# Six ring slots instead of eight, and one weight chunk of the gating unit kept for both token blocks

## The chip, the cores and the metric

One core of one Trainium2 chip runs the kernel. The time is the device time of one execution in microseconds. Before: 1674.19 us, the median of three runs (1673.43 to 1676.97).

## The reference

A decoder trunk of two layers on 256 tokens of width 1024, all in float32. Layer 0 mixes tokens by stick-breaking attention and gated linear attention, layer 1 by a gated unit; behind each stands a retrieval of single-neuron experts (PEER). Cut to what the change touches:

```python
def layer_c(h, w_in, v_norm, w_spatial, b_spatial, w_out):
    z = gelu(h @ w_in)                      # w_in: 1024 x 4096
    u, v = split(z, 2)
    v = rmsnorm(v, v_norm)                  # in chunks of 128 tokens, 8 groups
    mixed = einsum('gts,bnsgc->bntgc', causal(w_spatial), v) + b_spatial
    return (u * mixed) @ w_out

def peer(h, w_q, subkeys, u_tab, v_tab):
    ...                                     # 8 heads x top 16 = 128 experts per token: idx, gate
    act = gelu(einsum('td,tkd->tk', x, u_tab[idx]))
    return einsum('tk,tkd->td', gate * act, v_tab[idx])
```

Every token needs 128 rows of `u_tab` and 128 rows of `v_tab`, which the kernel keeps side by side as one row of 2048 floats.

## The kernel before

The 256 tokens are two blocks of 128, one token to a partition. The work stands in a list of stages, `PLAN` (line 191), which each engine walks in the same order and of which it takes its own part; semaphores join them.

**The gather loop.** A PEER of one block is 128 steps, four such loops in a row: layer 0 block 0, layer 0 block 1, layer 1 block 0, layer 1 block 1, in all 512 steps. In a step GpSimd issues an indirect DMA (line 543) that gathers one expert's row for each of the 128 tokens into a slot of `ring`, 128 x 2048 floats. VectorE multiplies the first half with `h` and sums (line 1043), ScalarE makes the gelu, scales it by the gate and writes a diagonal matrix (lines 718, 719, 721), and TensorE multiplies that with the second half of the slot into the accumulators `acc` (line 1363), which frees the slot (`rows_used`). The ring has `SLOTS` = 8 slots, and `dots`, `gelus` and `diag` have as many. GpSimd waits before step t until step t - 8 is used:

```python
if t >= SLOTS:
    pool.wait_ge(rows_used, t - SLOTS + 1)
```

**What runs between the steps.** `gather_with` (line 95) sets other stages behind given steps: behind the steps of layer 0 block 0 the query products of both blocks (`parts_of_layer0`), behind those of layer 0 block 1 the whole layer 1 trunk of block 0 (`trunk_for(0)`), behind those of layer 1 block 0 the trunk of block 1 and further query products (`trunk_for(1)`, `parts_for(0)`). TensorE does all this in its one queue with the gather's matmuls.

**The weights.** All weights come in chunks of 1024 x 512 floats, 128 x 4096 on the chip, into a double buffer `weights`, issued by SyncE (`load_chunk`, line 420): chunk n waits until chunk n - 2 has been used. The input weights of the gating unit are 8 chunks, `c_w_in[0]` to `c_w_in[7]`. A block uses them in the order 4, 5, 6, 7, 0, 1, 2, 3 (`ZPROJ` and `ZMORE` in `trunk_for`, TensorE's helper `tall`, line 1144), so each is loaded twice, once for each block: 16 loads. One chunk, the first of the query weights, lies in `z` instead (`first_chunk`), without the double buffer.

**The ring before the loops.** While layer 0 mixes, the ring's 8 x 2048 floats per partition hold its intermediate tiles (`slots(k)`, k = 0 to 15 in halves of a slot); the halves 12 to 15 hold `v_g`, `gg`, `og` and `scT`.

Of the kernel before, what the change touches and what calls it, by code (L numbers as in the profile page):

```python
# [19 lines left out]
NEG = -1.0e30  # L20
LOWEST = -3.0e38

SLOTS = 8
STEPS = NE
PARTS = 4
PHEADS = PH // PARTS
# [53 lines left out]
def chunks_of(kind, args):  # L80

    if kind == "QPROD":
        layer, b, m, heads = args
        return int(layer == 1 or (b == 0 and not first_chunk_holds(layer, m)))
    return {"PROJQK": 2, "PROJV": 1, "MIX0": 5, "ZPROJ": 1, "MIXO": 2}.get(kind, 0)


ALL = tuple(range(PHEADS))
# [30 lines left out]
def projected(at, layer, b, m, gap=2):  # L119

    q = (layer, b, m, ALL)
    done = at + gap * (TILES - 1) + 1
    return ([(at, ("QPROD", *q))] + [(at + gap * i, ("QMORE", *q, i)) for i in range(1, TILES)]
            + [(done, ("QTAKE", *q)), (done + 1, ("QDOT", *q)), (done + 3, ("DTAKE", *q))])
# [51 lines left out]

def parts_of_layer0():

    return (projected(0, 0, 0, 1) + projected(10, 0, 1, 1, 4) + ranked(11, 0, 0, 2, 2) + projected(16, 0, 0, 2)
            + ranked(23, 0, 0, 3, 2) + projected(26, 0, 1, 2, 4) + projected(33, 0, 0, 3) + ranked(36, 0, 0, 4, 2)  # L180
            + projected(46, 0, 1, 3, 4) + ranked(48, 0, 0, 5, 2) + projected(62, 0, 1, 0, 4) + ranked(60, 0, 0, 6, 2)
            + ranked(72, 0, 0, 7, 2) + ranked(84, 0, 1, 0, 2) + ranked(96, 0, 1, 1, 2) + ranked(108, 0, 1, 2, 2)
            + ranked(120, 0, 1, 3))
# [60 lines left out]
def trunk(nc, x_in, cols, gains, ab_w_in, ab_w_rank, ab_w_alpha2, ab_w_out, c_w_in, c_v_norm, c_spatial, c_w_out,  # L244
# [6 lines left out]
    with ctx:  # L251
# [9 lines left out]
        hT = sb("hT", [P, KT, T])  # L261
        mixT = sb("mixT", [P, KT, T])
        weights = sb("weights", [P, 2, KT, CH])
        ring = sb("ring", [P, SLOTS, 2 * D])
        z = sb("z", [P, 2 * SGW])
        scores = sb("scores", [P, 2 * PH * NK])
        scores1 = sb("scores1", [P, 2 * PH * NK])
# [36 lines left out]
        def slots(k, n=1):  # L304
            return ring[:, :, :].rearrange("p a b -> p (a b)")[:, k * D:(k + n) * D]

        first_chunk = z[:, :].rearrange("p (k n) -> p k n", n=CH)

        suffix = slots(9)[:, 768:768 + 2 * P].rearrange("p (a b) -> p a b", a=2)
# [28 lines left out]
        chunk_in = [sem(f"chunk_in{k}") for k in range(2)]  # L338
        half_used = sem("half_used")
        first_chunk_in = sem("first_chunk_in")  # L340
        out_full = sem("out_full")
        x_in_sem = [sem(f"x_in{b}") for b in range(NBLK)]
        consts_in = sem("consts_in")
# [67 lines left out]
        @block.sync  # L411
        def _(sp):
            norms = 0
            norms_with = {}
            chunk_free = []

            def filled(n):
                return full[n % WB], n // WB + 1

            def load_chunk(n, src, used):  # L420
                if n >= 2:
                    sp.wait_ge(*chunk_free[n - 2])
                sp.dma_start(weights[:, n % 2, :, :], src).then_inc(chunk_in[n % 2], 16)
                chunk_free.append(used)

            halves_used = 0
            for kind, args, at in walk():
                bank, chunk = at.bank, at.chunk
                if kind == "COLS":
                    sp.dma_start(consts[:, :], cols).then_inc(cols_in, 16)  # L430
                elif kind == "NORM":
                    name = args[0]
                    if name in GAIN_SLOT and name not in norms_with:
                        if name == "final":
                            sp.wait_ge(h_ready, norms_with["ffn0"])
                        src = gains[("ffn0", "ffn1", "final").index(name)]
                        slot = GAIN_SLOT[name][0]
                        sp.dma_start(gain[:, slot, :], src.partition_broadcast(P)).then_inc(gain_in[slot], 16)
                    norms += len(args[1])
                    norms_with[name] = norms  # L440
                elif kind == "PROJQK":
                    for j in range(2):
                        load_chunk(chunk + j, ab_w_in[j], filled(bank + 2 * j + 1))
                    sp.dma_start(w_rank[:, :, :], ab_w_rank).then_inc(consts_in, 16)
                elif kind == "PROJV":
                    load_chunk(chunk, ab_w_in[2], filled(bank + 1))
                elif kind == "MIX0":
                    for j, (part, last) in enumerate(((3, B_GK), (5, B_GG1), (4, B_GV1))):
                        load_chunk(chunk + j, ab_w_in[part], filled(bank + last))
                    for n in range(2):  # L450

                        load_chunk(chunk + 3 + n, ab_w_out[n], (out_full, 3 + n))
                elif kind == "GLAREAD":
                    sp.wait_ge(*filled(bank + 1))
                    sp.dma_start(first_chunk, peer_w_q[0, 0]).then_inc(first_chunk_in, 16)
                elif kind == "SPATIAL":
                    sp.dma_start(spatialT[:, :, :], c_spatial).then_inc(spatial_in, 16)
                elif kind == "QKEYS":
                    if args[0]:
                        sp.wait_ge(*filled(BANKS["QDOT", 0, 1, 0, ALL]))  # L460
                    sp.dma_start(keysT[:, :, :], peer_keys[args[0]]).then_inc(keys_in, 16)
                elif kind == "QPROD" and not first_chunk_holds(args[0], args[2]):
                    layer, b, m, heads = args
                    if layer == 1:
                        load_chunk(chunk, peer_w_q[layer, m], filled(bank))
                    elif b == 0:
                        load_chunk(chunk, peer_w_q[layer, m], filled(BANKS["QPROD", layer, 1, m, heads]))
                elif (kind, *args) == ("VNORM", 0):
                    sp.dma_start(v_norm[:, :], c_v_norm.partition_broadcast(P)).then_inc(v_norm_in, 16)
                elif kind == "ZPROJ":  # L470
                    load_chunk(chunk, c_w_in[args[1]], filled(bank))
                elif kind == "MIXO":
                    halves_used += 1
                    for kh in range(2):
                        load_chunk(chunk + kh, c_w_out[kh, args[1]],
                                   filled(bank) if kh else (half_used, halves_used))
                elif kind == "FINISH":
                    for n in range(2):
                        sp.wait_ge(h_ready, norms + n + 1)
                        sp.dma_start(out[0, (NBLK - 1) * P:, n * CH:(n + 1) * CH], h[:, NBLK - 1, n * CH:(n + 1) * CH])\  # L480
                            .then_inc(stored, 16)
                elif kind == "STORE":
                    sp.wait_ge(h_ready, norms)
                    sp.dma_start(out[0, args[0] * P:(args[0] + 1) * P, :], h[:, args[0], :]).then_inc(stored, 16)
            sp.wait_ge(stored, 16 * (NBLK + 1))

        @block.gpsimd
        def _(pool):
# [32 lines left out]
            for kind, args, at in walk():  # L521
# [14 lines left out]
                elif kind == "GATHER":  # L536
                    layer, b, i0, i1 = args
                    for step in range(i0, i1):
                        t = first_step(layer, b) + step
                        pool.wait_ge(experts_ready, 1 + IDS_ORDER[layer, b, step // TOPK])  # L540
                        if t >= SLOTS:
                            pool.wait_ge(rows_used, t - SLOTS + 1)
                        pool.indirect_dma_start(  # L543
                            ring[:, step % SLOTS, :], None, uv_rows,
                            bass.IndirectOffsetOnAxis(ap=experts[:, b, step:step + 1], axis=0))\
                            .then_inc(row_in[step % SLOTS], 16)

        @block.scalar
        def _(act):
# [108 lines left out]
            for kind, args, at in walk():  # L658
# [54 lines left out]
                elif kind == "GATHER":  # L713
                    layer, b, i0, i1 = args
                    for step in range(i0, i1):
                        k = step % SLOTS
                        act.wait_ge(dots_done, first_step(layer, b) + step + 1)
                        link(nc.scalar.activation(gelus[:, k:k + 1], dots[:, k:k + 1], ACT.Gelu))  # L718
                        link(nc.scalar.activation(gelus[:, k:k + 1], gelus[:, k:k + 1], ACT.Copy,  # L719
# [35 lines left out]
        def _(dve):  # L755
# [216 lines left out]
            for kind, args, at in walk():  # L972
# [64 lines left out]
                elif kind == "GATHER":  # L1037
                    layer, b, i0, i1 = args
                    for step in range(i0, i1):
                        k = step % SLOTS  # L1040
                        t = first_step(layer, b) + step
                        dve.wait_ge(row_in[k], 16 * (t // SLOTS + 1))
                        nc.vector.tensor_tensor_reduce(  # L1043
# [58 lines left out]
        def _(pe):  # L1102
# [40 lines left out]

            def tall(n, chunk, src, b, q=0, pieces=1):

                wt = await_chunk(pe, chunk)
                w = work[n % WB] if q else claim_bank(pe, n)
                for k in range(q * KT // pieces, (q + 1) * KT // pieces):
                    last = nc.tensor.matmul(w[:, :], src[:, k, b * P:(b + 1) * P], wt[:, k, :],  # L1149
# [150 lines left out]
            for kind, args, at in walk():  # L1300
# [56 lines left out]
                elif kind == "GATHER":  # L1357
                    layer, b, i0, i1 = args
                    for step in range(i0, i1):
                        pe.wait_ge(diag_ready, first_step(layer, b) + step + 1)  # L1360
                        k = step % SLOTS
                        for n in range(2):
                            last = nc.tensor.matmul(acc[2 * b + n][:, :], diag[:, k, :],  # L1363
                                                    ring[:, k, D + n * CH:D + (n + 1) * CH],
                                                    start=False, stop=True, skip_group_check=True)
                        last.then_inc(rows_used, 1)
                elif kind == "ZPROJ":
                    tall(bank, chunk, hT, args[0], 0, Z_PIECES)
                elif kind == "ZMORE":
                    tall(bank, chunk, hT, args[0], args[2], Z_PIECES)  # L1370
                elif kind == "MIXG":
                    b, k = args
                    pe.wait_ge(spatial_masked, 1)
# [57 lines left out]
```

## Time and profile before

| | before |
|---|---|
| median of 3 runs | 1674.19 us |
| the profiled execution's own time | 1672.77 us |
| span of its trace | 1671.0 us |
| TensorE matmul busy | 1440.7 us, 86% |
| VectorE busy | 983.1 us, 59% |
| ScalarE busy | 681.5 us, 41% |
| GpSimd busy | 658.7 us, 39% |
| moved by DMA | 637.54 MB, mean 382 GB/s |
| granted TensorE clock, mean | 0.969 of full speed |

The span runs from the first to the last instruction of the program; the profiled execution's time lies 1.8 us above it. A busy share is an average over stages with different limits. The share of the DMA engines is a mean over the core's 16 engines.

### The profile page before, as it was taken

How to read it: one execution, taken by the hardware profiler on the slowest of the kernel's cores; microseconds unless marked ns; L12 is line 12 of the kernel's file. 1: busy time of each engine (PE TensorE's matmuls, PEld its weight loads, DVE VectorE, ACT ScalarE, POOL GpSimd, SP SyncE). 2: the span in 40 equal slices, each digit the busy share in tenths (PEclk: the TensorE clock that was granted, in tenths of full speed). 3: DMA queues.
4: the chain of work that ended last, by engine and by line, in shares of the span. 5: the costliest groups of instructions: out<-in, count | busy, mean ns of one | idle time of the engine just before them, and what ended most of it. 6: DMA issues, size and time to landing. Idle time of an engine off the chain costs nothing.

```text
span 1671.0 us, 14524 instructions
## 1 busy us (share of the span) xinstructions
PE 1440.7 (86%) x4326; PEld 705.8 (42%) x4326; DVE 983.1 (59%) x2484; ACT 681.5 (41%) x1854; POOL 658.7 (39%) x537
## 2 busy tenths in 40 slices
PE   6999799998777988998888897989888897897786
PEld 5665466653222333443334444444334343342222
DVE  1132666776778755643446755664554785777654
ACT  1672334453345534333334433533334452544433
POOL 1000244464464433344244342424333553445673
PEclk9999799999899999999999999999999998999999
DMA  5323799999999999999999999999999999999996
GB/s 205 112 101 113 294 369 421 412 422 423 421 422 421 423 421 423 420 423 423 421 421 422 391 422 421 398 401 394 422 422 422 421 420 424 421 421 421 421 421 263
DMA packets 82190, 637.54 MB, mean 382 GB/s; under 512 B 9264, under 2 KB 9408, under 8 KB 10560
## 3 DMA queue, kind: packets, MB, share of 16 engines
q0 software_dynamic: 73728, 536.90, 77.8%
q1 hardware_dynamic: 8064, 98.65, 14.3%
q10 hardware_dynamic: 320, 1.07, 0.2%
q8 instruction: 34, 0.56, 0.1%
q14 instruction: 44, 0.36, 0.1%
HBM read 635.53 MB, written 1.05 MB: 381 GB/s over the span
## 4 chain that ended last, share of the span: by engine, by line
PE 41%; DMA 38%; DVE 8%; ACT 5%; issue 5%; POOL 4%; DVEq 0%; POOLq 0%; ACTq 0%
DMA ring<-in_peer_uv,experts 35%; PE acc L1363 22%; PE work L1149 7%; PE work L1164 6%; DVE ring L1043 4%; POOL ring L543 4%; PE work L1139 2%; PE acc L1328 1%; DMA weights<-in_c_w_in 1%; ACT diag L721 1%; ACT gelus L719 1%; DMA weights<-in_peer_w_q 1%; PE work L1347 1%; DMA x<-in_x 1%; ACT gelus L718 1%
## 5 line engine op out<-in xcount | busy, mean ns | idle before, releaser
L1363 PE MATMUL acc<-ring,diag 128*128 128x512 f32 x2048 | 983.2, 616 | 181.1 <-ACT diag L721 179.6
L543 POOL DMA_INDIRECT ring<-in_peer_uv,experts x512 | 648.8, 1267 | 872.7 <-PE acc L1363 721.7
L1043 DVE CUSTOM_DVE_ANT_0 ring<-ring,h 128x1024 f32<-128x1024 f32 x512 | 625.5, 1226 | 466.8 <-DMA ring<-in_peer_uv,experts 458.2
L1363 PEld LDWEIGHTS acc<-ring,diag 128*128 128x128 f32 x2048 | 373.8, 194 | 717.7 <-ACT diag L721 371.3
L718 ACT ACTIVATE gelus<-dots 128x1 f32<-128x1 f32 x512 | 103.0, 201 | 681.9 <-DVE dots L1043 681.0
L721 ACT ACTIVATE diag<-ident,gelus 128x128 f32<-128x128 f32 x512 | 205.6, 401 | 16.7
L1149 PE MATMUL work<-weights,hT 128*128 128x512 f32 x352 | 168.5, 611 | 12.0 <-DMA weights<-in_c_w_in 12.0
L719 ACT ACTIVATE gelus<-gelus,gates 128x1 f32<-128x1 f32 x512 | 150.8, 295 | 16.6
L1164 PEld LDWEIGHTS work<-hT,weights 128*128 128x128 f32 x896 | 109.8, 194 | 28.1 <-issue 26.4
L1164 PE MATMUL work<-hT,weights 128*128 128x128 f32 x896 | 109.9, 277 | 0.9 <-DMA weights<-in_peer_w_q 0.9
L1149 PEld LDWEIGHTS work<-weights,hT 128*128 128x128 f32 x352 | 68.2, 198 | 93.3 <-issue 80.1
L1178 PE MATMUL work<-weights,mixT 128*128 128x512 f32 x128 | 62.7, 614 | 0.0
L718 ACT ACT_TABLE_LOAD x38 | 48.8, 1283 | 0.7
L1139 PE MATMUL work<-hT,weights 128*128 128x256 f32 x192 | 42.0, 380 | 1.1 <-DVE hT L986 1.1
L532 POOL TENSOR_SCALAR_AFFINE_SELECT ring<-ring 128x512 f32<-128x512 f32 x2 | 1.3, 631 | 105.3 <-ACT ring L608 105.3
L1043 DVE DVE_READ_ACCUMULATOR2_ANT dots<- 128x1 f32 x512 | 42.3, 83 | 0.0
L712 ACT ACT_TABLE_LOAD x32 | 41.1, 1283 | 0.6
L1178 PEld LDWEIGHTS work<-weights,mixT 128*128 128x128 f32 x128 | 25.6, 200 | 32.9 <-issue 32.9
L1139 PEld LDWEIGHTS work<-hT,weights 128*128 128x128 f32 x192 | 36.3, 190 | 6.1 <-issue 1.4
L703 ACT ACTIVATE queries<-work 128x512 f32<-128x512 f32 (+1 forms) x17 | 9.7, 572 | 69.3 <-PE work L1164 69.2
L736 ACT ACTIVATE z<-work 128x512 f32<-128x512 f32 x16 | 9.6, 597 | 53.9 <-PE work L1149 53.9
L1328 PE MATMUL acc<-weights,mixT 128*128 128x512 f32 x64 | 28.7, 597 | 1.5 <-DVE mixT L995 0.8
(173 smaller groups left out, 749.1 us busy)
## 6 DMA issues: line engine op xcount, KB each, us to landing
weights<-in_c_w_in SPq DMA_DIRECT2D x16, 2048.0 KB, 11.9
weights<-in_peer_w_q SPq DMA_DIRECT2D x11, 2048.0 KB, 11.5
weights<-in_c_w_out SPq DMA_DIRECT2D x8, 2048.0 KB, 11.8
weights<-in_ab_w_in SPq DMA_DIRECT2D x6, 2048.0 KB, 8.3
ring<-in_peer_uv,experts POOLq DMA_INDIRECT x512, 14.8
weights<-in_ab_w_out SPq DMA_DIRECT2D x2, 2048.0 KB, 7.8
keysT<-in_peer_keys SPq DMA_DIRECT2D x2, 1024.0 KB, 9.5
z<-in_peer_w_q SPq DMA_DIRECT2D x1, 2048.0 KB, 7.8
```

The lines of the kernel that those rows point to most:

```text
L543: pool.indirect_dma_start(ring[:, step % SLOTS, :], None, uv_rows, bass.IndirectOffsetOnAxis(ap=experts[:, b, step:step + 1], axis=0))\
L712: nc.scalar.activation(g, g, ACT.Exp).then_inc(gate_exp, 1)
L718: link(nc.scalar.activation(gelus[:, k:k + 1], dots[:, k:k + 1], ACT.Gelu))
L719: link(nc.scalar.activation(gelus[:, k:k + 1], gelus[:, k:k + 1], ACT.Copy, scale=gates[:, b, step:step + 1]))
L721: nc.scalar.activation(diag[:, k, :], ident[:, :], ACT.Copy, scale=gelus[:, k:k + 1])\
L1043: nc.vector.tensor_tensor_reduce(out=ring[:, k, 0:D], in0=ring[:, k, 0:D], in1=h[:, b, :], scale=1.0, scalar=0.0, op0=ALU.mult, op1=ALU.ad ...
L1139: last = nc.tensor.matmul(dst, wt[:, k, t * P:(t + 1) * P], hT[:, k, cols], start=(k == 0), stop=(k == KT - 1))
L1149: last = nc.tensor.matmul(w[:, :], src[:, k, b * P:(b + 1) * P], wt[:, k, :], start=(k == 0), stop=(k == KT - 1))
L1164: last = nc.tensor.matmul(w[:, i * P:(i + 1) * P], wt[:, k, t * P:(t + 1) * P], hT[:, k, b * P:(b + 1) * P], start=(k == 0), stop=(k == KT ...
L1178: last = nc.tensor.matmul(w[:, :], mixT1[:, k, :], wt[:, k % KT, :], start=(k == 0), stop=(k == 2 * KT - 1))
L1328: last = nc.tensor.matmul(acc[2 * b + n][:, :], mixT[:, k, b * P:(b + 1) * P], wt[:, k, :], start=(k == 0), stop=(k == KT - 1))
L1363: last = nc.tensor.matmul(acc[2 * b + n][:, :], diag[:, k, :], ring[:, k, D + n * CH:D + (n + 1) * CH], start=False, stop=True, skip_group ...
```

## The change

The ring has six slots, and the room of the other two, halves 12 to 15, becomes `kept_chunk`. The input weight chunk 4 is loaded into it once, in a new stage `KEEP` of SyncE, and stays there for both blocks; the 14 other loads go on through the double buffer. Slots are counted by the step's number over all four loops, since 128 is not a multiple of 6. The last buffers get shorter: `diag`, `dots` and `gelus` have six slots.

```diff
-SLOTS = 8
+SLOTS = 6
+KEPT_SLOTS = 2
+KEPT = 4
...
+    if kind == "ZPROJ":
+        return int(args[1] != KEPT)
+    return {"PROJQK": 2, "PROJV": 1, "MIX0": 5, "MIXO": 2}.get(kind, 0)
...
-    return (projected(0, 0, 0, 1) + projected(10, 0, 1, 1, 4) + ranked(11, 0, 0, 2, 2) + projected(16, 0, 0, 2)
+    return ([(40, ("KEEP",))] + projected(0, 0, 0, 1) + projected(10, 0, 1, 1, 4) + ranked(11, 0, 0, 2, 2) + projected(16, 0, 0, 2)
...
-        ring = sb("ring", [P, SLOTS, 2 * D])
+        ring = sb("ring", [P, SLOTS + KEPT_SLOTS, 2 * D])
...
+        kept_chunk = slots(2 * SLOTS, 2 * KEPT_SLOTS).rearrange("p (k n) -> p k n", n=CH)
...
-                elif kind == "ZPROJ":
+                elif kind == "KEEP":
+                    sp.wait_ge(*filled(BANKS["QDOT", 0, 0, 1, ALL]))
+                    sp.dma_start(kept_chunk, c_w_in[KEPT]).then_inc(kept_chunk_in, 16)
+                elif kind == "ZPROJ" and args[1] != KEPT:
                     load_chunk(chunk, c_w_in[args[1]], filled(bank))
...
-                            ring[:, step % SLOTS, :], None, uv_rows,
+                            ring[:, t % SLOTS, :], None, uv_rows,
...
-                        k = step % SLOTS
+                        k = (first_step(layer, b) + step) % SLOTS
...
+            def z_piece(n, chunk, b, j, q=0):
+
+                if j == KEPT:
+                    pe.wait_ge(kept_chunk_in, 16)
+                    tall_of(n, kept_chunk, hT, b, q, Z_PIECES)
+                else:
+                    tall(n, chunk, hT, b, q, Z_PIECES)
...
                 elif kind == "ZPROJ":
-                    tall(bank, chunk, hT, args[0], 0, Z_PIECES)
+                    z_piece(bank, chunk, *args)
                 elif kind == "ZMORE":
-                    tall(bank, chunk, hT, args[0], args[2], Z_PIECES)
+                    z_piece(bank, chunk, *args)
```

`KEEP` stands at step 40 of the first loop, but SyncE walks the list ahead of the other engines: its wait, for a product of the query stage before, is long over when it gets there. SyncE's queue around it, before (the names are destination and source, in brackets the semaphore that is waited for; `bank_full` counts finished products, and with its last product a chunk has been used):

```order
L423 DMA weights<-in_peer_w_q 128x4096 [waits out_full] x2
L423 DMA weights<-in_peer_w_q 128x4096 [waits bank_full1]
L461 DMA keysT<-in_peer_keys 128x2048 [waits bank_full0]
L423 DMA weights<-in_c_w_in 128x4096 [waits bank_full1] x2
L423 DMA weights<-in_c_w_in 128x4096 [waits bank_full3]
L423 DMA weights<-in_c_w_in 128x4096 [waits bank_full0]
L469 DMA v_norm<-in_c_v_norm 128x2048
```

And with the change:

```order
L429 DMA weights<-in_peer_w_q 128x4096 [waits out_full] x2
L429 DMA weights<-in_peer_w_q 128x4096 [waits bank_full1]
L478 DMA ring<-in_c_w_in 128x4096 [waits bank_full0]
L467 DMA keysT<-in_peer_keys 128x2048 [waits bank_full0]
L429 DMA weights<-in_c_w_in 128x4096 [waits bank_full1] x2
L429 DMA weights<-in_c_w_in 128x4096 [waits bank_full0]
L475 DMA v_norm<-in_c_v_norm 128x2048
```

One load of `c_w_in` is now behind the third query chunk, into the ring's room, and one of the four before `v_norm` is gone. The second place in SyncE's queue is block 1's trunk, before:

```order
L423 DMA weights<-in_peer_w_q 128x4096 [waits bank_full0]
L423 DMA weights<-in_c_w_in 128x4096 [waits bank_full3]
L423 DMA weights<-in_c_w_in 128x4096 [waits bank_full1]
L423 DMA weights<-in_c_w_in 128x4096 [waits bank_full0]
L423 DMA weights<-in_peer_w_q 128x4096 [waits bank_full2]
```

And with the change:

```order
L429 DMA weights<-in_peer_w_q 128x4096 [waits bank_full0]
L429 DMA weights<-in_c_w_in 128x4096 [waits bank_full3]
L429 DMA weights<-in_c_w_in 128x4096 [waits bank_full1]
L429 DMA weights<-in_peer_w_q 128x4096 [waits bank_full2]
```

Chunks 4, 5 and 6 were loaded there; now it is 5 and 6, and the load that waited for chunk 4's last product is gone. On TensorE, VectorE, ScalarE and GpSimd the instructions and their order are the same.

## Rows read from the trace of the kernel before

**Rows 1.** The page: the span, the gathers' queue and the weight chunks' issues.
```profile
span 1671.0 us, 14524 instructions
...
q0 software_dynamic: 73728, 536.90, 77.8%
...
weights<-in_c_w_in SPq DMA_DIRECT2D x16, 2048.0 KB, 11.9
```
**Rows 2.** Busy time by stretch: start:end, length, busy us per engine, PEclk, DMA share, GB/s.
```profile
209.00:225.00 16.00, 16.00 (x76) 10.27 (x75) 6.17 (x10) 2.04 (x7) 5.74 (x7) 0.99 0.85 308
225.00:267.00 42.00, 42.00 (x196) 26.54 (x195) 32.11 (x91) 18.12 (x54) 18.66 (x17) 1.00 1.00 412
...
345.00:541.00 196.00, 156.38 (x407) 65.69 (x406) 146.02 (x404) 84.73 (x243) 101.26 (x74) 0.97 1.01 422
541.00:595.00 54.00, 50.51 (x118) 21.57 (x117) 38.10 (x100) 24.34 (x68) 22.31 (x20) 0.97 1.01 422
595.00:941.00 346.00, 299.76 (x744) 133.47 (x742) 186.21 (x427) 130.93 (x378) 132.54 (x113) 0.97 1.01 422
941.00:968.00 27.00, 26.96 (x110) 15.96 (x111) 18.31 (x44) 12.49 (x35) 9.33 (x8) 1.00 0.95 369
968.00:1000.00 32.00, 30.21 (x71) 12.86 (x70) 20.66 (x52) 12.74 (x35) 13.66 (x12) 1.00 1.01 423
...
1030.00:1066.00 36.00, 29.51 (x80) 13.97 (x78) 15.95 (x46) 14.84 (x39) 9.66 (x9) 0.91 1.00 391
...
1120.00:1133.00 13.00, 13.00 (x55) 7.70 (x54) 7.91 (x19) 3.57 (x8) 3.74 (x4) 0.97 0.77 294
...
1153.00:1177.00 24.00, 23.78 (x61) 10.85 (x59) 15.96 (x48) 10.57 (x29) 10.70 (x9) 1.00 1.01 423
```
**Rows 3.** Who waited for whom: total us, times, longest.
```profile
POOL ring L543 <- PE acc L1363: 721.7, 350, 16.0
```
**Rows 4.** Instructions in order of time, a gather's dot, its matmuls, GpSimd's next issue: start, us, instruction.
```profile
452.35 1.23 DVE L1043 CUSTOM_DVE_ANT_0 ring<-ring,h 128x1024 f32<-128x1024 f32 x1 [1.14 <-DMA ring<-in_peer_uv,experts]
...
454.63 1.98 PE L1363 MATMUL acc<-ring,diag 128*128 128x512 f32 x4 [0.39 <-ACT diag L721]
...
457.39 1.96 POOL L543 DMA_INDIRECT ring<-in_peer_uv,experts  x1 [1.44 <-PE acc L1363]
```
**Rows 5.** Gathers from issue to landing, 355 to 541 us, then 1120 to 1134 us.
```profile
DMA to landing us min/median/max: 12.9/14.8/26.9
...
DMA to landing us min/median/max: 5.4/6.5/12.9
```
**Rows 6.** SyncE's issues in order of time (xN: as many in that stretch).
```profile
266.79 0.33 SPq L423 DMA_DIRECT2D weights<-in_peer_w_q  x1
...
400.45 202.12 SPq L423 DMA_DIRECT2D weights<-in_c_w_in  x4
...
886.66 88.15 SPq L423 DMA_DIRECT2D weights<-in_c_w_in  x3
```
**Rows 7.** GpSimd in order of time, the start of the first gather loop.
```profile
190.43 1.73 POOL L543 DMA_INDIRECT ring<-in_peer_uv,experts  x1 [0.30 <-issue]
208.12 0.94 POOL L543 DMA_INDIRECT ring<-in_peer_uv,experts  x1 [15.97 <-PE acc L1363]
212.64 1.33 POOL L543 DMA_INDIRECT ring<-in_peer_uv,experts  x1 [3.58 <-PE acc L1363]
```
**Rows 8.** GpSimd in order of time, 1020 to 1066 us.
```profile
1044.50 0.93 POOL L543 DMA_INDIRECT ring<-in_peer_uv,experts  x1 [13.15 <-PE acc L1363]
```
**Rows 9.** The chain that ended last, 1095 to 1180 us: start, us, what.
```profile
1105.71 11.47 DMA weights<-in_c_w_in
...
1177.55 20.45 DMA ring<-in_peer_uv,experts
```
**Rows 10.** GpSimd in order of time, 1095 to 1185 us.
```profile
1110.75 1.24 POOL L543 DMA_INDIRECT ring<-in_peer_uv,experts  x1 [0.78 <-PE acc L1363]
1123.41 1.06 POOL L543 DMA_INDIRECT ring<-in_peer_uv,experts  x1 [11.41 <-PE acc L1363]
...
1130.79 0.94 POOL L543 DMA_INDIRECT ring<-in_peer_uv,experts  x1 [3.98 <-PE acc L1363]
1132.50 0.94 POOL L543 DMA_INDIRECT ring<-in_peer_uv,experts  x1 [0.78 <-PE acc L1363]
```

More of the change, by code:

```diff
@@ L84, in chunks_of @@
         return int(layer == 1 or (b == 0 and not first_chunk_holds(layer, m)))
-    return {"PROJQK": 2, "PROJV": 1, "MIX0": 5, "ZPROJ": 1, "MIXO": 2}.get(kind, 0)
+    if kind == "ZPROJ":
+        return int(args[1] != KEPT)
+    return {"PROJQK": 2, "PROJV": 1, "MIX0": 5, "MIXO": 2}.get(kind, 0)
 ALL = tuple(range(PHEADS))
@@ L340, in trunk @@
         first_chunk_in = sem("first_chunk_in")
+        kept_chunk_in = sem("kept_chunk_in")
         out_full = sem("out_full")
@@ L543, in _ @@
                         pool.indirect_dma_start(
-                            ring[:, step % SLOTS, :], None, uv_rows,
+                            ring[:, t % SLOTS, :], None, uv_rows,
                             bass.IndirectOffsetOnAxis(ap=experts[:, b, step:step + 1], axis=0))\
-                            .then_inc(row_in[step % SLOTS], 16)
+                            .then_inc(row_in[t % SLOTS], 16)
         @block.scalar
@@ L1039, in _ @@
                     for step in range(i0, i1):
-                        k = step % SLOTS
+                        k = (first_step(layer, b) + step) % SLOTS
                         t = first_step(layer, b) + step
@@ L1144, in tall, with tall_of @@
             def tall(n, chunk, src, b, q=0, pieces=1):
-                wt = await_chunk(pe, chunk)
+                tall_of(n, await_chunk(pe, chunk), src, b, q, pieces)
+            def z_piece(n, chunk, b, j, q=0):
[4 more added lines that the diff above has]
+                    tall(n, chunk, hT, b, q, Z_PIECES)
+            def tall_of(n, wt, src, b, q, pieces):
                 w = work[n % WB] if q else claim_bank(pe, n)
@@ L1360, in _ @@
                         pe.wait_ge(diag_ready, first_step(layer, b) + step + 1)
-                        k = step % SLOTS
+                        k = (first_step(layer, b) + step) % SLOTS
                         for n in range(2):
```

## The prediction

> **What bounds the kernel now.** I read the page first. Nearly everything after 180 us is a loop of 512 gathers: 536.90 MB in 512 issues is 1.049 MB each, and a weight chunk is 2048 KB, 2.097 MB [rows 1]. Then the busy times by stretch [rows 2]. In 345 to 541 and in 595 to 941 the DMA engines are busy without a break (share 1.01) at 422 GB/s, while PE works 156 of 196 us and 300 of 346: the transfers are the bound, a gather costs 1.049/422 = 2.485 us, a chunk 4.97 us. In 209 to 267 PE is busy all the time (16.00 of 16, 42.00 of 42), and in 941 to 968 and 1120 to 1133 again: there PE is the bound, the landed rows wait for it in the ring, and the DMA share falls to 0.85, 0.95 and 0.77. So the kernel changes between two bounds, and the ring is what lets the transfers run ahead while PE is late.
>
> How far they may run ahead is set by GpSimd: it waits 721.7 us in 350 waits for PE's matmul that frees a slot [rows 3]. What a slot needs beyond its transfer: one gather whose dot starts at 452.35, as soon as it landed, has its matmuls from 454.63 on for 1.98 us [rows 4], so it is free at 456.6, 4.3 us after the landing, and GpSimd's next issue stands at 457.39, 0.8 us later. In 355 to 541 a gather lands 14.8 us after its issue (median), but 5.4 us is enough when little is queued [rows 5]. Eight slots at 2.485 us are 19.9 us a round, 4.3 + 0.8 + 14.8: the 14.8 is mostly queue. Six slots are 14.9 us a round, which leaves 9.8 us for the landing, above 5.4. So where the transfers are the bound and nothing is late, **six slots cost nothing**; a delay of the consumer that is longer than about 9.8 - 5.4 = 4.4 us (9.4 with eight) lets the DMA engines go idle.
>
> **The change, part by part.**
>
> Compute: every engine does the same instructions in the same order, apart from slot numbers; PE waits for another semaphore before the products with chunk 4. Cost 0.
>
> Traffic: one chunk of 2.097 MB less, 4.97 us if the transfers are the bound where it is dropped. Where is that? For block 0 nothing is saved: chunk 4 used to be loaded in the pair issued from 400.45, and the two loads there are now chunks 5 and 6; chunk 4 is loaded behind the query chunk issued at 266.79 [rows 6], and a later load near 581 goes. Between the two the DMA engines are busy without a gap, so all work in between is 5 us later, and comes back at 581. In 541 to 595 PE is busy 50.51 of 54 us [rows 2], so a part may not come back: 0 to 2.5 us lost, I take **+0.5**.
>
> For block 1 the three loads from 886.66 on [rows 6] become two, so 4.97 us of transfers go between 956 and 990. There PE is busy 26.96 of 27 us and then 30.21 of 32 [rows 2]: at most 1.8 us of waiting can go in these two windows, and 4.97 if the lead pays later. I take **-2** (bounds 0 and -5), since PE is nearer to being the bound.
>
> Start: GpSimd issues eight gathers, the last at 190.43, and stands idle 15.97 us until PE frees the first slot, issue at 208.12, then 212.64 [rows 7]. With six slots it stops two gathers earlier and issues the seventh at that same 208.12, because PE gets the first rows as before. From there each instant of issue carries a gather whose number is two lower. PE hides that while it is the bound; when the transfers become the bound, near 345, the program stands two gathers further back: 2 x 2.485 = **+5.0**. Could it be less? The transfers ran at 412 GB/s in 225 to 267 [rows 2]; at 422 they would win back 1 us there, and as much again up to 345, nearly one gather: bounds 2.5 and 5, and I take 5, since the issue instants stay what they are.
>
> The wait near 1030: PE stands still for a chunk, GpSimd for 13.15 us, until 1044.50 [rows 8]. With eight slots the DMA share of 1030 to 1066 is still 1.00, at 391 GB/s [rows 2], since two chunk loads are in flight too. With six the last two gathers that fill this hole are missing; the gathers issued from 1044.5 on come in pairs, 5.4 us at least behind their issue. Between nothing (the chunk loads fill it) and two gathers, 5.0: I take the middle, **+2.5**. The Trainium skill ("DMA: Bandwidth & Descriptors", the fit of fixed and variable time) gives a transfer about 2.0 us fixed plus bytes at 436 GB/s, an estimate of 4.4 us for one gather; the row here says 5.4 at best [rows 5], and the measurement is what I use. By the page's figure the hole would be about 1 us shorter and the sum 1 us lower.
>
> 1105 to 1177: PE waits for the chunk issued at 1105.71 for most of 11.47 us, and the chain comes back to a gather at 1177.55 [rows 9]. The eight gathers are all issued by 1110.75; the next issues are at 1123.41, 1130.79 and 1132.50 [rows 10], and the DMA share of 1120 to 1133 is 0.77: the ring of eight already ran dry. It is the start again: from here each issue carries a gather two lower, while what else is loaded is the same, and behind 1153 the DMA share is 1.01 [rows 2]. So **+5.0** (bounds 2.5 and 5).
>
> The rest: behind 1177 the transfers are the bound to the end. Delays above 4.4 us on VectorE or PE while a block's trunk stage ends can bite where eight slots hid them: 0 to 2.5, I take **+1**.
>
> Sum: 0.5 - 2 + 5 + 2.5 + 5 + 1 = **+12 us** on the profiled execution's 1672.8, so 1684.8; I say 1685, which also stands for the median (1674.2 before, 1.4 above the profiled one). All lower ends together: 0 - 5 + 2.5 + 0 + 2.5 + 0 = 0. All upper ends: 2.5 + 0 + 5 + 5 + 5 + 2.5 = +20.
>
> **The rivals.**
>
> *Faster: the cushion is not worth its two gathers.* Where the ring is full, PE is the bound by definition; if it still is when the transfers have lost their two gathers, or catches its next chunk wait first, the loss vanishes in PE's own time. Place: 209 to 345 and 1120 to 1177. Then both terms of 5.0 go and the dropped chunk counts whole: 1672.8 - 5 = 1668. It decides from the point on where PE is busy 100% up to the next chunk wait. For it: PE is busy 42.00 of 42 us. Against it: the DMA share is 1.00 in those same windows, so nothing there can catch up, and long stretches bound by transfers follow both.
>
> *Wash.* The losses are half of what I take and the dropped chunk counts whole: +7 - 5, 1671 to 1676. For it: each loss was taken near its upper end.
>
> *Much slower: four gathers in the queue are too few in the long stretches as well.* The gelu and top-k work on ScalarE and VectorE, or a spell at the lower TensorE clock, holds a slot for more than 4.4 us beyond the least often enough. Against it: the shortest landing in 355 to 541 is 12.9 us [rows 5], two gathers' time less is 7.9, still above 5.4. Price: if one in a hundred of the 1,070 us of these stretches is lost, 11 us more: 1696.
>
> *The change does not do what it says.* If the load of chunk 4 into the ring's room had to wait for its last user, PE would stand; but that room is free since the mixing of layer 0, before the first gather, and the load is issued some 300 us before its use. I give it nothing.
>
> **How the numbers follow.** Forecast 0.55, wash 0.17, faster rival 0.13, much slower 0.15. Measurements of this kernel tell about 0.2%, 3.3 us. The forecast and the much slower case are slower; the wash is mostly within 0.2% but has a part at its upper edge: faster 0.13, same 0.15, slower 0.72. The range takes the lower end of the sum and the wash, and the upper end up to the much slower case: 1671 to 1695.
>
> **What would show it.** In the profile after: 8 gathers' issues before GpSimd's long wait at the start become 6, and the next stands again near 208; median landing in the long stretches near 9.8 us instead of 14.8, at a DMA share still of 1.01; a stretch around 1120 to 1135 with a lower DMA share than 0.77; the dropped bytes, 2.1 MB, in the total; and between 345 and 580 each point of the program about 10 us later than before, 5 of it given back near 590. I am wrong if the long stretches move less than 420 GB/s (much slower), or if the kernel is no later at 345 than the 5 us of the moved chunk (faster rival).

## The result, and the profile after

The change takes 1701.54 us (median of six runs, 1699.32 to 1708.71) against 1674.49 us before (six runs, 1673.09 to 1676.97): 27 us slower, ratio 1.0162, 95% interval 1.0146 to 1.0179. The forecast was 1685.0, range 1671 to 1695: the direction was right, but the 11 us foretold are less than half of the 27 measured, and the measured time lies 6.5 us above the range.

The page of the changed kernel, the rows that answer to [rows 1]:

```profile
span 1698.3 us, 14525 instructions
...
DMA packets 82046, 635.44 MB, mean 374 GB/s; under 512 B 9248, under 2 KB 9392, under 8 KB 10544
...
q0 software_dynamic: 73728, 536.90, 77.2%
```

2.10 MB less were moved, as the change says, in 27 us more. Who waited for whom, in the changed kernel (line 552 is the gather, 1052 the dot, 1383 the gather's matmuls):

```profile
POOL ring L552 <- PE acc L1383: 735.9, 361, 19.2
ACT gelus L727 <- DVE dots L1052: 723.0, 415, 6.6
DVE ring L1052 <- DMA ring<-in_peer_uv,experts: 508.6, 327, 7.3
```

GpSimd waits 736 us for a slot instead of 722 [rows 3], and VectorE waits 509 us for landings; before, that was 458 us. Busy times by stretch, changed kernel (columns as in [rows 2]; 1136 to 1151 is about the place in the program that was 1120 to 1133 before):

```profile
209.00:225.00 16.00, 16.00 (x72) 10.51 (x71) 4.69 (x8) 3.47 (x12) 5.47 (x6) 0.95 0.76 279
225.00:267.00 42.00, 40.93 (x184) 25.04 (x183) 30.10 (x83) 18.14 (x53) 20.05 (x16) 1.00 0.98 393
267.00:345.00 78.00, 71.21 (x315) 42.99 (x313) 48.12 (x131) 31.70 (x89) 29.66 (x27) 0.98 0.98 394
...
1136.00:1151.00 15.00, 15.00 (x53) 8.13 (x53) 8.17 (x19) 3.57 (x8) 3.21 (x4) 0.89 0.56 215
```

The row of the kernel before that [rows 2] does not show:

```profile
267.00:345.00 78.00, 77.84 (x334) 46.98 (x334) 56.20 (x154) 39.74 (x112) 36.75 (x31) 1.00 1.01 417
```

TensorE no longer works without a gap between 225 and 345 us: 6.8 us of gaps in 267 to 345 alone, where before it was busy 77.84 of 78. And the stretch in which the DMA engines go idle behind the chunk wait, 0.77 before, is now 0.56. The start is as foretold: GpSimd issues six gathers, the last at 189.69, and stands until the first slot is free, at 209.88 (foretold 208.12; this trace is 1.8 us behind already when its first gather is done).

```profile
189.69 0.94 POOL L552 DMA_INDIRECT ring<-in_peer_uv,experts  x1 [0.30 <-issue]
209.88 0.94 POOL L552 DMA_INDIRECT ring<-in_peer_uv,experts  x1 [19.25 <-PE acc L1383]
214.22 0.93 POOL L552 DMA_INDIRECT ring<-in_peer_uv,experts  x1 [3.41 <-PE acc L1383]
```

The other signs that the prediction named: the long stretches run at a DMA share of 1.01, but they move 416 GB/s in 372 to 558 us and 420 in 612 to 958, where the kernel before had 422. So the sign given for the much slower case, under 420, did appear, while the lag (below) stands still at 17 us in the first of these stretches: it was too fine a sign. Landing times of gathers are not in the trace of the changed kernel. The kernels of the experiments with other numbers of slots have them, and the prediction's sum, slots x 2.485 less the 5.1 (4.3 + 0.8) between landing and next issue, holds: in 355 to 541 us the median landing is 9.7 us with six slots (without the loads), 12.2 with seven, 14.8 with eight and 19.7 with ten, where the sum gives 9.8, 12.3, 14.8 and 19.8.

**Where the time came from.** Both kernels do the same 512 gathers in the same order, so I compared the time at which gather n's last matmul ends in the two traces. The lag grows like this (from the matmul records, gathers counted from 0, each lag a difference of two times, one trace of each kernel):

| gathers | before, us | lag of the change at the end | grown by | foretold |
|---|---|---|---|---|
| up to 8 (layer 0's mixing) | to 229 | 1.6 | +1.6 | 0 |
| 8 to 64 | to 369 | 16.9 | +15.3 | +10 (5 ring, 5 moved load) |
| 64 to 168 | to 667 | 11.7 | -5.2 | -4.5 (the moved load comes back) |
| 168 to 264 | to 960 | 12.9 | +1.2 | 0 |
| 264 to 280 | to 1004 | 10.6 | -2.3 | -2 (block 1's load dropped) |
| 280 to 312 | to 1123 | 18.5 | +7.9 | +2.5 |
| 312 to 336 | to 1194 | 24.1 | +5.6 | +5 |
| 336 to 511 | to 1664 | 27.2 | +3.1 | +1 |

Two rows carry most of the error, 8 to 64 with 5.3 us and 280 to 312 with 5.4 us of 15.2 in all. The granted clock is no explanation of the sum: its mean is 0.970 in this trace and 0.969 in the one before. The chain of the changed kernel in the first of them (start, us, what):

```profile
268.21 3.57 PE work L1184 x32
271.79 1.73 PE acc L1383 x4
274.28 15.64 DMA ring<-in_peer_uv,experts
292.19 1.28 ACT L721
```

A gather issued at 274.28 lands 15.64 us later and TensorE waits for it. The two weight loads, the third query chunk and the kept chunk, were issued at 270.03 and 270.40; the kept chunk landed at 289.7. What the queues moved in 275 to 279 us (queue, packets, MB, share of the 16 engines):

```profile
q1 hardware_dynamic: 67, 1.10, 64.0%
q0 software_dynamic: 76, 0.61, 36.2%
```

q0 are the gathers, q1 the weight loads: 67 packets of 16 KB against 76 of 8 KB, about one of each in turn. The gathers get 0.61 MB in 4 us, so one lands every 7 us, while TensorE takes one every 2.56 in the kernel before (gather 0 ends at 207.3, gather 56 at 350.7). The Trainium skill ("DMA: Bandwidth & Descriptors", queues, rings and completion order, on arbitration) says that an engine goes round the queues packet by packet; the trace agrees as far as its counts can show it, 67 and 76 packets in these 4 us.

### The profile page after: what moved, and what is told of

The parts are those of the page before. It is cut to its first block, busy times and chain, and to the rows that moved or that the text cites. A ratio compares the mean times of both kernels' runs of the same rounds, so it can differ in the third digit from the quotient of the medians.

```text
span 1698.3 us, 14525 instructions
## 1 busy us (share of the span) xinstructions
PE 1446.9 (85%) x4326; PEld 704.3 (41%) x4326; DVE 983.7 (58%) x2484; ACT 682.6 (40%) x1854; POOL 666.2 (39%) x537
## 4 chain that ended last, share of the span: by engine, by line
PE 39%; DMA 35%; DVE 10%; ACT 6%; issue 5%; POOL 4%; POOLq 0%; DVEq 0%; ACTq 0%
DMA ring<-in_peer_uv,experts 32%; PE acc L1383 21%; PE work L1169 6%; DVE ring L1052 5%; PE work L1184 5%; POOL ring L552 4%; PE work L1148 2%; PE acc L1348 1%; DMA weights<-in_c_w_in 1%; ACT diag L730 1%; ACT gelus L728 1%; PE work L1198 1%; DMA weights<-in_peer_w_q 1%; ACT gelus L727 1%; DMA x<-in_x 1%
## 5 line engine op out<-in xcount | busy, mean ns | idle before, releaser
L552 POOL DMA_INDIRECT ring<-in_peer_uv,experts x512 | 656.3, 1282 | 895.6 <-PE acc L1383 735.9
L1169 PE MATMUL work<-weights,hT 128*128 128x512 f32 x320 | 152.8, 611 | 11.1 <-DMA weights<-in_c_w_in 11.1
L728 ACT ACTIVATE gelus<-gelus,gates 128x1 f32<-128x1 f32 x512 | 150.8, 295 | 16.6
L1169 PEld LDWEIGHTS work<-weights,hT 128*128 128x128 f32 x320 | 61.5, 197 | 84.1 <-issue 71.8
```

What stands on the lines that cost most here:

```text
L552: pool.indirect_dma_start(ring[:, t % SLOTS, :], None, uv_rows, bass.IndirectOffsetOnAxis(ap=experts[:, b, step:step + 1], axis=0))\
```

## The experiments

The theories, as they stood behind the result. A: a weight load in flight makes a gather's landing long, and six slots do not cover it where TensorE is the bound. B, my prediction: two gathers at each place where the ring was full. C: the kept chunk itself does the harm. Later A was made sharper as R, and D (six slots are too few whether or not weights are loaded) and S (a load takes too large a share of the traffic) were added. Every trace is of one execution.

**six_slots_only.** The change without the kept chunk.

```diff
-    return ([(40, ("KEEP",))] + projected(0, 0, 0, 1)
+    return (projected(0, 0, 0, 1)
...
-                elif kind == "ZPROJ" and args[1] != KEPT:
+                elif kind == "ZPROJ":
...
-                if j == KEPT:
+                if False:
```

> The change without the kept chunk: six slots, chunk 4 loaded twice through the double buffer as before, the room of the other two slots unused. Theory A (a gather takes 13 to 16 us to land while weight loads are in flight, however few gathers are queued, and six slots do not cover that in stretches where TensorE is the bound): most of the 27 us is here, 18 to 25 us slower than before, without the 9 us step near 290 us and without the gain of 5 us near 590. Theory B (my prediction: two gathers, 5 us, at each of the two places where the ring was full): 13 to 15 us slower, and the rest of the 27 comes from the kept chunk. Theory C (the kept chunk's load or its reading from the ring's room does the harm): under 8 us slower.

Measured 1708.16 us against 1675.48: ratio 1.0189 (1.0167 to 1.021), 33 us slower. So the ring alone costs at least what the change costs, more than the 18 to 25 us that A gave it, and by the medians the kept chunk gives 6 us back, though the two intervals overlap. B and C fall. Its lag at gather 64 is 13.5 us although no second load is in flight there, and between gathers 264 and 280, where the change gains 2.3, it loses 4.9: by these two traces the dropped load is worth 7 us there, more than its 4.97 us of transfers. The profiled execution was the slowest of the four (1711.44 us; its lag at the end is 38.7 instead of 32.7), so these 7 us are not firm.

**six_slots_keep_late.** The kept chunk's load moved.

```diff
-    return ([(40, ("KEEP",))] + projected(0, 0, 0, 1)
+    return (projected(0, 0, 0, 1)
...
-    out = [(0, ("QKEYS", 1))] if b == 0 else []
+    out = [(0, ("QKEYS", 1)), (0, ("KEEP",))] if b == 0 else []
```

> The change, with the kept chunk's load moved behind the load of layer 1's keys (near 417 us, where the transfers are the bound and gathers queue), instead of behind the third query chunk near 270 us. Theory A: the step of 8.8 us at gathers 28 to 30 goes; 4 to 9 us faster than the change, 18 to 23 us slower than before. Theory B: the transfers are the same in sum, within 2 us of the change.

Measured 1700.45 us, ratio 1.0139 (1.0115 to 1.0164): the interval overlaps that of the change. By gather, the lag at 32 is 8.3 instead of 12.1, as A says, but at 96 it is 18.7: the load costs its 5 us near 420 instead, and hardly comes back near 590: the lag is 18.6 at gather 128 and 18.0 at 168, where the change went from 17.1 to 11.7. Why it stays was not tested. In sum there is nothing to tell: A's 4 to 9 us are a miss, B's "within 2 us of the change" holds.

**eight_slots_keep** and **eight_slots_keep_late.** Can both be had? The room for eight slots and the kept chunk comes from tiles whose lives do not overlap. The last norms' gains then share one tile, so a gain's load waits for the norm before; eight_slots_keep_late also has the edit of six_slots_keep_late.

```diff
-SLOTS = 6
+SLOTS = 8
...
-        scores1 = sb("scores1", [P, 2 * PH * NK])
-        gain = sb("gain", [P, 2, D])
+        gain = sb("gain", [P, 1, D])
...
-        w_alpha = sb("w_alpha", [RANK, GH * GDK])
-        w_rank = sb("w_rank", [P, KT, RANK])
+        w_alpha = v_norm[0:RANK, T:T + GH * GDK]
+        w_rank = v_norm[:, 512:512 + KT * RANK].rearrange("p (k n) -> p k n", n=RANK)
...
-        alphaT = sb("alphaT", [RANK, T])
+        alphaT = v_norm[0:RANK, 0:T]
...
+        scores1 = mixT[:, :, :].rearrange("p a b -> p (a b)")
```

> Eight slots and the kept chunk as well, its load near 267 us; the room comes from other tiles (the second score rows lie in mixT, one gain tile instead of two, three small tiles of layer 0 in v_norm's room; the squares' scratch of block 0 in the score rows). Nothing is left out. Theory A: two weight loads in flight at once near 270 us still cost 0 to 5 us with eight slots, the dropped load of block 1 gives 1 to 5 us: between 5 us faster and 2 us slower than before. Theory C: at least 8 us slower than before.

> As eight_slots_keep, with the kept chunk's load behind the keys' load near 400 us. Theory A: no stall near 270 us, the dropped load of block 1 gives 2 to 5 us: 2 to 5 us faster than before, and 0 to 4 us faster than eight_slots_keep. Theory B: 1 to 5 us faster than before, the same as eight_slots_keep.

Measured 1673.48 us, ratio 0.9983 (0.9972 to 0.9994), and 1674.04 us, 0.999 (0.9979 to 1.0001). With eight slots the kept chunk is worth 2 us by the medians (1.0 to 4.7 by the first interval, nothing certain by the second), less than its 4.97 us of transfers, and no difference by the place of its load can be told. A and B allowed this; C is out for good. No run has the moved tiles alone, so what they cost or give is inside these figures.

**eight_slots_no_loads** and **six_slots_no_loads.** No weight chunk is loaded behind the first ten, which leaves out 33 of the 43 loads into the double buffer (the 34 of the expectations is one too many); the products use what lies there.

```diff
             def load_chunk(n, src, used):
+                if n > 9:
+                    return
...
-            eng.wait_ge(chunk_in[n % 2], 16 * (n // 2 + 1))
+            m = n if n <= 9 else 8 + n % 2
+            eng.wait_ge(chunk_in[n % 2], 16 * (m // 2 + 1))
```

> The kernel before (eight slots) without the weight chunks that are loaded during the gather loops: from the third query chunk on no chunk is loaded and the products use what the double buffer holds, so the output is not the reference's. The gathers, the keys, the gains and all products stay. 25 chunk loads and more go, 34 x 4.97 = 169 us of transfers at most, but TensorE has about 1,440 us of work: I expect 1,530 to 1,580 us. It is the base line for six_slots_no_loads.

> The same with six slots and nothing kept, so the output is not the reference's either. Theory A (six slots are too few where weight loads are in flight): at most 10 us slower than eight_slots_no_loads, against 33 us between the kernels with their loads. Theory D (six slots are too few for the consumers' delays alone, loads or not): 20 us or more slower.

Measured 1559.75 and 1579.78 us, two runs each, and 1556.6 against 1573.2 us of span in the two traces. The two runs with six slots are 9.7 us apart (1574.93 and 1584.62), and the trace is of the faster. So six slots cost 16.6 us by the traces and 20.0 by the medians without any load in the loops: A's 10 is a miss, D's 20 is met by the medians and not by the traces, and it is half of the 33 or somewhat more. By gather (lag of six behind eight): 6.4 us grow up to gather 66, 1.6 from there to 252, 3 us in 252 to 264, nothing to 372, 6 us in 372 to 420. The first is the two gathers of the start, which B put at 5.0. The other two lie at the turns behind gathers 256 and 384, where the add, norm and transposes of a block run beside the loop; that these are what holds the slots there is argued, not tested, and the turn behind gather 128 shows nothing. And nothing grows at gathers 264 to 336, where the kernels with loads lose 11 us (the change) and 18 us (six_slots_only).

**seven_slots** and **ten_slots**, later **nine_slots.** The price of a slot; nothing is kept (the edit of six_slots_only comes on top), all loads stay. Nine and ten have the room of eight_slots_keep, with its moved tiles.

```diff
-SLOTS = 6
-KEPT_SLOTS = 2
+SLOTS = 7
+KEPT_SLOTS = 1
```

> Seven slots, nothing kept, all loads as before. Theory A (a round of seven is covered in more of the stretches): the cost bends, 6 to 14 us slower than before where six slots are 33 us slower. Theory B (one gather less at each place where the ring was full): 7 us. A straight line through six slots would be 16 us.

> Ten slots, nothing kept, all loads as before; the room comes from the same other tiles as in eight_slots_keep. If the ring of eight was full at the start and near 1120 us, and each slot there is worth a gather, two more slots give up to 10 us; theory A, in which the cost of a missing slot falls with the number of slots: 3 to 10 us faster than before.

> Nine slots, nothing kept, room as in ten_slots. Between eight (0) and ten (-8 us): theory R, in which each slot is one gather of reserve and each further one is needed in fewer places: -4 to -7 us.

| slots, nothing kept | median, us | before, us | ratio (95%) | against before |
|---|---|---|---|---|
| 6 | 1708.16 | 1675.48 | 1.0189 (1.0167 to 1.021) | +32.7 |
| 7 | 1685.0 | 1675.4 | 1.0058 (1.0041 to 1.0075) | +9.6 |
| 9 | 1670.36 | 1674.53 | 0.998 (0.997 to 0.999) | -4.2 |
| 10 | 1667.33 | 1675.4 | 0.9949 (0.9932 to 0.9966) | -8.1 |

The curve bends: the seventh slot is worth 23 us, the eighth 10, the ninth and tenth 4 each. A's 6 to 14 us for seven and 3 to 10 for ten hold, and so does the -4 to -7 for nine; B's 7 us for seven lies at the edge of what was measured, and a straight line from six slots, 16 us, falls. Ten slots are the fastest kernel here that loads all its weights, 8 us below before and 34 below the change, in the room that the kept chunk would take beside eight. At the start its DMA engines have work throughout:

```profile
209.00:225.00 16.00, 16.00 (x71) 10.55 (x70) 8.31 (x15) 3.76 (x13) 5.76 (x5) 0.92 1.01 421
...
267.00:345.00 78.00, 77.84 (x348) 48.15 (x347) 56.33 (x152) 40.68 (x116) 32.81 (x32) 1.00 1.01 417
1120.00:1133.00 13.00, 13.00 (x58) 7.96 (x57) 5.65 (x14) 4.90 (x13) 3.94 (x4) 1.00 0.82 313
```

In 209 to 225 the DMA share is 1.01 where eight slots had 0.85 [rows 2]; near 1120 it is 0.82 against 0.77.

**six_slots_one_load** and **eight_slots_one_load.** Theory R says what a load costs: 5 us of transfers, which a loop bound by TensorE can bridge only with gathers that have already landed. The two kernels without loads get a single one back, the third query chunk, issued near 270 us; the other 32 stay out.

```diff
-                if n > 9:
+                if n > 10:
...
-            m = n if n <= 9 else 8 + n % 2
+            m = n if n <= 10 else 9 + (n + 1) % 2
```

> six_slots_no_loads with one weight load back in: the third query chunk, issued near 267 us, in the stretch from 209 to 345 us in which TensorE is the bound. The other 34 loads stay out, so the output is not the reference's. Theory R (a load is 5 us of transfers; where TensorE is the bound the loop can only bridge it with gathers that have already landed in the ring): with six slots there is no such reserve, so the lag behind eight_slots_one_load steps by 3 to 7 us between gathers 26 and 70, beyond the 5.9 us that six slots lose there without any load. Theory D (loads are nothing special): the lag stays at 5.9 us, within 1.5.

> eight_slots_no_loads with the same one load, for comparison gather by gather; the output is not the reference's. Theory R: eight slots hold two landed gathers more, which is the 5 us of one load: gathers 26 to 56 are at the same times as in eight_slots_no_loads, within 1 us, and at most 5 us later at gather 70, once the transfers are the bound.

| gather | 24 | 28 | 32 | 48 | 56 | 64 | 72 |
|---|---|---|---|---|---|---|---|
| six behind eight, no load, us | 0.6 | 0.6 | 0.7 | 1.7 | 4.6 | 5.8 | 5.9 |
| six behind eight, one load, us | 2.3 | 3.0 | 5.7 | 5.7 | 8.9 | 10.9 | 10.9 |
| eight with one load behind eight without, us | 2.5 | 2.5 | 2.5 | 2.5 | 2.5 | 2.5 | 2.5 |

Measured 1584.84 us with six slots and 1560.75 with eight, two runs each. With eight slots the load costs nothing: the 2.5 us are there from the first gathers on, before the load, and do not change. With six it costs 5.0 us at gather 64 and behind (10.9 against 5.9), or 4.7 counted as growth from gather 8: about one load's transfers. D foretold that the lag would stay at 5.9, so delays without loads are not the whole account. Two other traces with six slots and one load in this place agree: up to gather 64 their lag behind the kernel before grows by 11.5 us (six_slots_keep_late) and 12.9 (six_slots_only), where the pair without loads has 6.3. The whole times say less, since the two runs without loads lie 9.7 us apart. The chain of six_slots_one_load, then that of eight_slots_one_load, in the same stretch (L1384 and L1366 are the gather's matmuls, L1167 products of the query stage):

```profile
273.56 1.73 PE acc L1384 x4
275.29 0.02 issue
275.33 0.72 issue
276.05 10.24 DMA ring<-in_peer_uv,experts
```

```profile
276.60 3.44 PE acc L1366 x8
280.03 1.78 PE work L1167 x16
281.82 6.87 PE acc L1366 x16
288.69 1.78 PE work L1167 x16
```

The dots of the kernel with eight slots, in the same time:

```profile
276.18 1.23 DVE L1046 CUSTOM_DVE_ANT_0 ring<-ring,h 128x1024 f32<-128x1024 f32 x1 [2.97 <-DMA ring<-in_peer_uv,experts]
281.83 1.23 DVE L1046 CUSTOM_DVE_ANT_0 ring<-ring,h 128x1024 f32<-128x1024 f32 x1 [2.88 <-DMA ring<-in_peer_uv,experts]
284.20 1.23 DVE L1046 CUSTOM_DVE_ANT_0 ring<-ring,h 128x1024 f32<-128x1024 f32 x1 [1.15 <-DMA ring<-in_peer_uv,experts]
```

With six slots the chain waits for a gather that takes 10.24 us from its issue. With eight, too, a landing comes 5.65 us behind the last, but TensorE goes on with landed gathers. R holds at this place, within half a microsecond.

**change_half_loads.** Does the loads' large share of the traffic matter (theory S), or only their sum? Each chunk comes in two halves, so its rows have 8 KB, and the waits for a chunk count both halves.

```diff
-                sp.dma_start(weights[:, n % 2, :, :], src).then_inc(chunk_in[n % 2], 16)
+                for kh in range(2):
+                    ks = slice(kh * KT // 2, (kh + 1) * KT // 2)
+                    sp.dma_start(weights[:, n % 2, ks, :], src[:, ks, :]).then_inc(chunk_in[n % 2], 16)
```

> The change with each weight chunk (except the first query chunk, which lies in z) loaded by two DMAs of 8 KB a partition instead of one of 16 KB. In the profile of the change the chunk queue moves 1.10 MB and the gathers 0.61 MB in 4 us while a load is in flight, 67 packets to 76, so a packet of each in turn; with 8 KB rows it should be half and half, gathers landing every 5 us instead of 7.5 during a load and a chunk landing after 13 to 14 us instead of 11.5. Theory R: the transfers' work and so the stalls of gathers stay the same in sum, TensorE's waits for chunks grow by 2 us each: 0 to 8 us slower than the change. Theory S (what hurts is that a load takes two thirds of the traffic and starves the gathers): 5 to 15 us faster than the change, and the step at gathers 28 to 30 halves.

Measured 1706.6 us against 1674.53, ratio 1.0202 (1.0185 to 1.0219), where the change has 1.0162. The profile shows what it was to show, the queues in 279 to 283 us:

```profile
q1 hardware_dynamic: 111, 0.85, 50.9%
q0 software_dynamic: 111, 0.84, 50.0%
```

Half and half, one packet each in turn. Yet the lag that grows between gathers 24 and 32 is 7.4 us, after 8.9 in the change, not half; and TensorE's longest wait for a `c_w_in` chunk is 7.9 us instead of 5.6. So S falls, which wanted 5 to 15 us less than the change, and the 5 us more are within R's 0 to 8. The trace is of the fastest of five executions (1699.41 us), and what the doubled number of DMAs costs by itself was not separated.

## Why the prediction was wrong

**Bound by stretch, and the round of a slot**: right. In the long stretches bound by transfers the lag is flat, 17.2 us at gather 72 and 17.1 at 128, and 27.6 at 440 and 27.2 at the end. Six slots cost nothing there, the turn behind gather 384 apart (below).

**Start, +5.0**: right in kind, a little small. Without loads six slots lose 6.4 us up to gather 66, above the upper bound of 5.

**The step that failed** is the one behind it: that a delay up to 4.4 us is covered because "5.4 us is enough when little is queued", and that the ring's depth is paid for only where the ring was full and the DMA engines idle. I took the landing of a gather from 1120 to 1134 [rows 5] and did not ask how long it is with a weight load in flight, though in the same rows the longest was 12.9 us. TensorE is the bound from 209 to 345 us and takes a gather each 2.56 us; the transfers need 2.485, so they can win back less than 0.1 us a gather. A load of 4.97 us in such a stretch must be bridged by two landed gathers, and these were just the two slots that the change took. One load there costs six slots 4.7 to 5.0 us and eight slots nothing. The forecast has no term for it. The change makes it worse: it puts its kept chunk behind the third query chunk, into the one stretch of the first loop with nothing to spare. From gather 8 to 64 the lag grows 15.3 us, where 10 were foretold. By the traces it is made up of 6.3 for the ring without any load, some 5 to 6 for the third query chunk's load, which was there before (11.1 to 12.9 with it), and the rest, 2.4 to 4, for the moved load, which was put at 5.

**The wait near 1030, +2.5**: the mechanism stands, the size was off: 7.9 us from gather 280 to 312, with loads in flight for most of the time. The chain shows a gather of 13.32 us at 1071.92, as a chunk load is issued, and behind the wait for the query chunk TensorE comes back at the lower granted clock (3.79 us for 16 matmuls that take 1.78):

```profile
1008.04 12.23 DMA weights<-in_peer_w_q
1020.27 0.04 issue
1020.32 3.79 PE work L1184 x16
1024.10 2.99 PE work L1169 x4
...
1071.92 13.32 DMA ring<-in_peer_uv,experts
...
1087.54 3.39 PE acc L1383 x4
```

The kernel before has the wait too, but comes out of it at full clock:

```profile
996.89 11.54 DMA weights<-in_peer_w_q
...
1008.47 2.05 PE work L1164 x16
1010.52 1.72 PE work L1149 x4
```

TensorE stood idle 3.63 us right before these matmuls in the change and 0.87 before, and its granted clock in 1020 to 1027 us is 0.53, for the most part the lower level (1.2 GHz), where the kernel before had 1.00. The growth comes in two steps, 4.2 us at gathers 280 to 284 and 4.6 at 296 to 300. Of the first, 3.0 us are these 20 matmuls at the lower clock (3.79 + 2.99 against 2.05 + 1.72); in the second the matmuls behind the late gather take 3.39 us instead of 1.98. So an estimate from these rows is that some 4 of the 7.9 us come from a clock that is low behind TensorE's waits, a cost that the forecast had no term for. With eight slots it is caught up: eight_slots_keep comes out of the same wait with 3.42 us for the 16 matmuls, its lag goes from 0.4 to 2.4 us and is 0.5 again at gather 312. The condition itself is shown: in this place the lag grows 7.7 us in six_slots_only, 5.0 in six_slots_keep_late and 3.9 with seven slots, but 0.1 in eight_slots_keep and nothing between the kernels without loads. Whether the load in flight or TensorE's wait for the chunk does more was not separated.

**1105 to 1177, +5.0**: right, 5.6. **The moved load, +0.5 net**: right, it comes back near 590 (-5.2 against -4.5). **Block 1's load, -2**: right against the kernel before (-2.3), though six_slots_only, with the load in, loses 4.9 us there instead of nothing, for which the forecast has no reason. **The rest, +1**: 3.1 in the change in sum, of which 4.9 come in gathers 372 to 420, at the turn behind gather 384, and some is given back; and 9 us at the block turns in the kernels without loads: more than the 2.5 I gave as its upper end.

**The rivals.** The faster one and the wash needed TensorE's bound to hide the missing gathers; it hides them only until the next load. The faster one's 1668 also leaves out the other terms of its own sum, 0.5, 2.5 and 1, with which it would be 1672. The much slower one was nearest in size (1696). It expected the loss in the long stretches bound by transfers, where work of VectorE and ScalarE holds a slot for too long. Most of these stretches lose nothing, but the turn behind gather 384 lies in one and loses 5 to 6 us, so it was right in part.

## What to carry to other kernels

A buffer between two engines that are almost equally fast is a reserve, and what it must bridge is every transfer that is thrown in between, not only the stretches in which it is seen full or empty. Count, for each stretch in which the consumer is the bound, what else is moved there, in units of one slot's transfer, and read a landing time with the traffic that it will meet. Here room was worth more as slots of a ring that runs dry (4 us a slot, even beyond eight) than as a kept weight that saves 5 us of transfers and gives back 2.

## What was not expected of the hardware

Two queues share the DMA engines by packets, not by bytes: a weight load with 16 KB rows got 1.10 MB in 4 us beside 0.61 MB of gathers with 8 KB rows, and half (0.85 to 0.84 MB) once its rows were 8 KB. A wait that grows by 3 us can cost as much again, when TensorE comes out of it at the lower granted clock, as near 1020 us. Up to the first gather, in layer 0's mixing, which no experiment changes but the ones with moved tiles and change_half_loads (2.3 us ahead of the kernel before), the traces lie up to 2.9 us behind the kernel before (0.4 in six_slots_only, 2.8 in six_slots_keep_late); so a lag by gather should be read as growth, not as a level.
